# A mixed expert phase on one core: fewer gathered steps beside the choices and the one-hot blocks, more beside the dense part

## What is computed

```python
qry = x @ w_query                                   # 8 heads, two halves of 128
sc = qry . sub_keys                                 # 2 x 128 scores per head
s_top, i_top = top_k(sc, 16)                        # 16 per half
best_s, pos = top_k(s_top[0][:, None] + s_top[1][None, :], 16)   # 16 of 256
idx = i_top[0] * 128 + i_top[1] at pos              # 16 experts of 16384, per head
g = softmax(best_s)
out = sum_k g_k * gelu(expert_u[idx_k] . x) * expert_v[idx_k]    # 128 experts per token
```

## Time and profile before

| | us |
|---|---|
| median of 3 runs | 4753.62 (4751.6 to 4756.91) |
| the profiled execution | 4752.96 |
| its span in the trace | 4751.2 |

### The profile page before, as it was taken

The page is one execution under the profiler, slowest core; times in us unless marked ns, Lnnn a source line. Parts: engine busy times, 40 slices in busy tenths (PEclk is TensorE's granted clock), DMA queues, the critical chain, the costliest instruction groups (busy, mean ns, idle before and its releaser), DMA issues.

```text
span 4751.2 us, 61482 instructions
## 1 busy us (share of the span) xinstructions
PE 4023.7 (85%) x22629; PEld 2075.0 (44%) x22629; DVE 2817.4 (59%) x7082; ACT 1179.1 (25%) x3076; POOL 1241.0 (26%) x1018
## 2 busy tenths in 40 slices
PE   7786699996999989979864444589999999999998
PEld 3444444443777754434321222334444444444443
DVE  1323865775888867634668888735454554545434
ACT  0221111221555531121213544711111111111111
POOL 0201322222344223301332233322222222222221
PEclk9888799998999999989875767799999999999999
DMA  6143498986444377646898988999998999889996
GB/s 239 66 173 120 165 360 301 372 334 234 158 165 185 136 305 297 263 182 254 340 356 320 364 336 348 367 341 344 364 362 323 363 359 362 336 335 346 355 359 249
DMA packets 351291, 1370.43 MB, mean 288 GB/s; under 512 B 26896, under 2 KB 112528, under 8 KB 231568
## 3 DMA queue, kind: packets, MB, share of 16 engines
q0 software_dynamic: 129024, 939.58, 50.8%
q1 hardware_dynamic: 161840, 389.17, 22.4%
q10 hardware_dynamic: 60128, 37.75, 2.5%
HBM read 1277.22 MB, written 89.18 MB: 288 GB/s over the span
## 4 chain that ended last, share of the span: by engine, by line
PE 34%; DVE 11%; DMA 7%; issue 3%; ACT 2%; POOL 0%; SPq 0%; DVEq 0%; ACTq 0%; POOLq 0%
PE prompt_exp_wk L2309 13%; PE prompt_exp_wk L2325 11%; PE prompt_exp_acc L2289 6%; DVE prompt_exp_junk L2155 4%; DMA prompt_exp_ring<-in_experts_dram,prompt_exp_idx 3%; PE prompt_exp_wk L2239 3%; DMA gates_dram<-prompt_exp_area 2%; ACT prompt_exp_diag L1991 1%; DVE prompt_exp_topi L2052 1%; DVE prompt_exp_hit L2101 1%; DVE prompt_exp_hT L2139 1%; DVE prompt_exp_top L2049 1%; DMA scores_dram<-prompt_exp_area 1%; DVE prompt_exp_rest L2057 0%; POOL prompt_exp_ring L1894 0%
## 5 line engine op out<-in xcount | busy, mean ns | idle before, releaser
L1894 POOL DMA_INDIRECT prompt_exp_ring<-in_experts_dram,prompt_exp_idx x640 | 686.8, 1073 | 1977.6 <-PE prompt_exp_acc L2289 1758.0
L2155 DVE CUSTOM_DVE_ANT_0 prompt_exp_junk<-prompt_exp_ring,prompt_exp_h 128x1024 bf16<-128x1024 f32 x640 | 761.2, 1221 | 112.2 <-DMA prompt_exp_ring<-in_experts_dram,prompt_exp_idx 112.1
L2309 PE MATMUL prompt_exp_wk<-prompt_exp_hT,prompt_exp_area 128*128 128x384 f32 x2048 | 692.1, 492 | 16.2 <-DMA prompt_exp_area<-in_u_turned_dram 16.2
L2325 PE MATMUL prompt_exp_wk<-prompt_exp_area 128*128 128x512 f32 x1536 | 698.2, 603 | 0.0
L2289 PE MATMUL prompt_exp_acc<-prompt_exp_ring,prompt_exp_diag 32*32 32x512 f32 x10240 | 414.4, 677 | 225.2 <-ACT prompt_exp_diag L1991 224.0
L2190 DVE TENSOR_TENSOR prompt_exp_area<-prompt_exp_area,prompt_exp_wk 128x512 f32<-128x512 f32 x186 | 127.6, 686 | 776.9 <-PE prompt_exp_wk L2325 755.6
L537 PE MATMUL prompt_proj_acc<-normed_w,normed_hT 128*128 128x512 f32 x1280 | 553.8, 595 | 14.4 <-PEq L91 14.4
L2309 PEld LDWEIGHTS prompt_exp_wk<-prompt_exp_hT,prompt_exp_area 128*128 128x128 f32 x2048 | 385.0, 191 | 343.5 <-issue 88.4
L152 POOL DMA_INDIRECT sample_hid_ring<-in_experts_dram,sample_hid_idx x256 | 275.1, 1075 | 898.3 <-DVE sample_hid_acc L182 849.3
L2325 PEld LDWEIGHTS prompt_exp_wk<-prompt_exp_area 128*128 128x128 f32 x1536 | 283.8, 191 | 409.5 <-issue 378.3
L1984 ACT ACTIVATE prompt_exp_ge<-prompt_exp_dot 128x2 f32<-128x2 f32 x320 | 64.8, 203 | 1301.9 <-DVE prompt_exp_dot L2155 1301.4
(11 more groups left out here) (350 smaller groups left out, 5001.5 us busy)
## 6 DMA issues: line engine op xcount, KB each, us to landing
prompt_exp_area<-in_u_turned_dram SPq DMA_DIRECT2D x128, 512.0 KB
prompt_exp_area<-in_experts_dram SPq DMA_DIRECT2D x64, 1024.0 KB
gates_dram<-prompt_exp_area ACTq DMA_DIRECT2D x12, 2048.0 KB, 25.0
prompt_exp_area<-gates_dram SPq DMA_DIRECT2D x32, 768.0 KB, 10.7
sample_proj_w<-in_w_all_dram SPq DMA_DIRECT2D x10, 2048.0 KB, 20.0
normed_w<-in_w_all_dram SPq DMA_DIRECT2D x10, 2048.0 KB, 18.6
proj_dram<-prompt_proj_stage SPq DMA_DIRECT2D x80, 256.0 KB
prompt_exp_ring<-in_experts_dram,prompt_exp_idx POOLq DMA_INDIRECT x640
```

The costliest lines, as they stand in the source:

```text
L1894: nc.gpsimd.indirect_dma_start(out=ring[:, s % RING, :], out_offset=None, in_=experts, in_offset=bass.IndirectOffsetOnAxis(ap=idx[:, n % 2 ...
L2155: nc.vector.tensor_tensor_reduce(out=junk[:, s % 2, :], in0=ring[:, s % RING, 0:D], in1=h2[:, n % 2, :], scale=1.0, scalar=0.0, op0=ALU.mu ...
L2309: last = nc.tensor.matmul(wk[:, j % 2, 0:TURNED], ut[:, j % 3, k, :], hT_dense[:, k, :], start=(k == 0), stop=(k == KD - 1))
L2325: last = nc.tensor.matmul(wk[:, 2 + o % 2, :], act_e[:, c % 2, j, t * P:(t + 1) * P], vt[:, half, j, :], start=(j == 0), stop=(j == JB - 1))
```

## The change

Three places of `Turns.walk` advance by less:

```diff
             if v >= 13:
-                self.advance(2)
+                self.advance(1 + v % 2)
...
             for k in range(HEADS):
                 self.pick_dense(first + d + 1, k)
-                blocks(2)
-                self.advance(2 if k % 2 else 1)
-                blocks(2)
-                self.advance(2)
+                for _ in range(2):
+                    blocks(2)
+                    self.advance(1)
         turned(2)
-        for k in range(BLOCKS // 2):
-            blocks(2)
+        for k in range(BLOCKS // 4):
+            blocks(4)
             self.advance(1)
```

## The result

The changed kernel takes 4599.99 us (median of 4 runs, 4594.02 to 4604.45) against 4752.61 us of the kernel before (median of 4): a ratio of 0.9679, 95% interval 0.9662 to 0.9695. That is 153 us or 3.2% faster, where 17 us slower was forecast. The profiled execution has a span of 4599.3 us and a mean granted clock of 0.933.

The account below looks back on a forecast made before the run. TensorE was taken to bound the dense part, the DMA after the change, and VectorE to be nearest to full in B, C and D. 4752.96 - 157 + 174 gave 4770 us, range 4690 to 4840.

Parts of the forecast that it names:

- What bounds the kernel now: TensorE nearest to full in the dense part F, DMA close behind; VectorE in C and D, 182 of 210 us each.
- What the early stretches give back: Stretches A to E, ahead of the dense part F, lose 45 steps and get 157 us shorter.
- upper ends: Largest gains in the early stretches: A 49, B 53, E 34 us; C and D add all 28 idle us each.
- What the dense part pays: F takes the 45 moved steps and grows by 174 us, its chunk going from 50.75 to 56.2 us.
- so the bound changes over: In F steps wait for rows and TensorE behind them, so the DMA at 364 GB/s sets the chunk, 56.2 us.
- rival 2: TensorE stays the bound in F: F +52 to +60, 4648 to 4656 us, needing 390 GB/s; chance 0.06.
- The hand-overs: In F, four instead of three; each drops DMA to 66 GB/s for 10 us, set against a fuller queue.
- Rival 1: In F the DMA carries more than 367 GB/s: F +140 to +80, 4736 to 4676 us; chance 0.25.
- Rivals 3 and 4: 3: F's DMA gives about 350 GB/s, 4842 us, chance 0.15; 4: early stretches give only 116 us, 4811 us, chance 0.09.
- The Trainium skill's rule: HBM gives one core about 358 GB/s: a chunk would take 57.1 us, F +204, the kernel 4800 us.
- What would show it: Signs of a right forecast: L1950's last copy near 2828, C and D near 177 and 162 us, F's products every 56 us.

Follow-up runs that it names:

- half runs: Kernel before with gathers of 4 KB rows instead of 8 KB, with dots over 512 of 1024 elements, or with both: 4679.1, 4692.6, 4580.5 us.
- b_half_rows: Kernel before with gathers of 4 KB rows instead of 8 KB, engine work unchanged: 4679.1 us against 4759.4.
- last_only: Kernel before with only the last of the three edits, 10 steps instead of 18 in E, 8 more in F: 4736.9 us, ratio 0.9967.
- pace60: 60 steps ahead of the dense part instead of the changed kernel's 85: 4634.2 us, ratio 0.9758 to the kernel before.
- pace43: 43 steps ahead of the dense part instead of the changed kernel's 85: 4636.5 us, ratio 0.9755 to the kernel before.
- walk_only: Kernel before with only the first edit, 29 and 10 steps in A and B instead of 38 and 14, 13 more in F: 4702.3 us, ratio 0.9895.

## Why the prediction was wrong

- **What bounds the kernel now** was right for F. For C and D "VectorE is nearest to full" was read as "VectorE paces them". The half runs show two near bounds, VectorE and the DMA, one behind the other, and waits for gelu behind both.
- **What the early stretches give back**, 157 us, measured 217. The term was mis-sized in A (26, measured 50), C (33, 44), D (48, 64) and E (14, 34), and the other way in B (36, 28), where VectorE's idle time did not shrink. It priced the work that leaves and kept most of the idle time. Yet VectorE's idle time fell from 29 to 9 us in C and from 28 to 6 in D; the "upper ends", which the prediction set aside, were nearly right in D (69) and E (34). In A the upper end, 49, was met too, but by luck: it was the DMA time of 9 pairs, while half of the gain was TensorE's busy time, most of it with the clock, which the prediction left out. In E the two store stalls were counted as ScalarE's own, and half rows and `last_only` both show that they come from the DMA's backlog.
- **What the dense part pays**, 174 us, measured 65. This is the step that failed and decided the sign: "so the bound changes over", at a rate of 364 GB/s. TensorE's price of 52.4 us a chunk and the 390 GB/s that go with it were right: 52.5 us and 393 GB/s were measured, and with rows of half the size the chunk stayed at 52.3, so the bound did not change over. The 364 was what the DMA *had been asked for* in a stretch paced by TensorE; asked for more it gave 398 to 405. The share of 0.96 beside it looked like a nearly full DMA and was no measure: per unit of share the kernel before moved 350 / 0.92 = 380 GB/s in F, the changed one 393 / 0.98 = 401. In the queue rows of the profile's page too the same gathers come out faster in the changed kernel:

```profile
q0 software_dynamic: 129024, 939.58, 51.5%
```

  That is 939.58 MB / (0.515 x 4599 us) = 397 GB/s, where the earlier trace rows gave 389, and from that 389 rival 2 was called nearly impossible.
- **The hand-overs**, set off against a better queue, cost F nothing beyond the 4.4 us that TensorE's price has for the fourth: the chunk is at that price.
- **The rivals.** Rival 2, TensorE stays the bound in F, is what happened; it had 0.06. Its 4648 us are 48 too many: the early term is 60 short, and F took 13 more than its 52. Rival 1 (late rows keep four pairs waiting in the ring, so the DMA always has work) has its place in `pace60` and `pace43`, with a higher rate than it named; in the changed kernel the DMA does not hold F. Rivals 3 and 4 are wrong.
- **The Trainium skill's rule** ("DMA: Bandwidth & Descriptors", "Where 436 GB/s comes from"), about 358 GB/s from HBM for a core, which that section gets by halving a stack's 716 between two cores, does not hold here: 393 GB/s over 1.6 ms in the changed kernel, 405 in `pace43`, with the other cores at rest.
- **What would show it**: the last copy at L1950 was forecast near 2828, measured 2788; C and D at 177 and 162 us, measured 168 and 144; E above 100, measured 87; the chunk at 56, measured 52.5; TensorE's busy share at 0.93, measured 0.97, the sign given for rival 2; VectorE's waits for rows at 100 or more, measured 103, but TensorE's for the diagonal blocks at 100 to 200, measured 32.5. The last of these is the one that tells whether the rows are late.

## What to carry to other kernels

The best rate in a trace is a floor for a resource's ceiling, not the ceiling, wherever another engine sets the pace; before a sign is hung on it, measure the ceiling with a version that asks for too much. Where VectorE and the DMA were each busy for some 0.9 of a stretch, a step that used both was worth more than its price on VectorE, because waits between the engines left with it. Work that can lie in one of several stretches belongs where it costs one engine's time only (here 1.3 us a step beside the dense part against 4.6 beside the blocks), up to the knee at which that stretch's second resource fills.

## What was not expected of the hardware

- The DMA held 405 GB/s over 1.8 ms with gathers of 8 KB rows and loads mixed. Its mean share says little about what is left: it read 0.98 at 372 GB/s and at 393.
- Storing gates on ScalarE's queue takes it 0.37 us, but 8.4 us in stretch E of the kernel before, at a DMA share of 0.98 (12.5 once in `walk_only`), and ScalarE's work behind it waits. At shares of 0.80 (`b_half_rows`) to 0.95 (`pace43`) in E no such stall is left.
- VectorE is busy for less than half of F, and halving its dots still took 38 us off F.
